# Order of the input projections of a state-space block in a one-core kernel

## The reference, cut to what is computed

```python
zxbcdt = rms_norm(x, ln_g) @ in_w                      # 1024 -> 2048 (z) + 3072 (x, B, C) + 32 (dt)
xbc = silu(causal_dwconv(xbc, conv_w, conv_b))         # 4 taps
y = ssd_chunked(xs * dt, a, bm, cm) + xs * d_skip      # 4 groups of 8 heads, 4 chunks of 128 tokens
y = y * silu(z)                                        # the gate
y = rms_norm(y per group) * norm_g
return y @ out_w
```

## Time and profile before

| | us |
|---|---|
| median of 3 runs (2411.29 to 2411.45) | 2411.38 |
| the profiled execution, device time | 2413.46 |
| its span, from first to last instruction | 2411.7 |
| TensorE busy in the span | 2383.3 |
| VectorE, ScalarE, GpSimd busy | 1404.2, 1054.0, 370.6 |

### The profile page before, as it was taken

The page is one execution under the profiler, slowest core; times in us unless marked ns, Lnnn a source line. Parts: engine busy times, 40 slices in busy tenths (PEclk is TensorE's granted clock), DMA queues, the critical chain, the costliest instruction groups (busy, mean ns, idle before and its releaser), DMA issues.

```text
span 2411.7 us, 29936 instructions
## 1 busy us (share of the span) xinstructions
PE 2383.3 (99%) x11690; PEld 1940.0 (80%) x11690; DVE 1404.2 (58%) x2203; ACT 1054.0 (44%) x1808; POOL 370.6 (15%) x296
## 2 busy tenths in 40 slices
PE   8999999999999999999999999999999999999998
PEld 6677778888888877788888787787788887888887
DVE  6878775763665677766456547535555445443342
ACT  6654564442445677644234334324443333322223
POOL 0352252210111000221011100001211001110001
PEclk9999999999999999999999999999999999999999
DMA  4542223223323221232332332231244322223322
GB/s 163 107 94 79 81 70 101 90 87 110 97 78 128 71 71 54 78 105 90 99 100 83 122 102 74 71 109 58 71 131 127 114 97 88 88 94 100 103 82 85
DMA packets 74270, 226.21 MB, mean 94 GB/s; under 512 B 8081, under 2 KB 12305, under 8 KB 74001
## 3 DMA queue, kind: packets, MB, share of 16 engines
q1 hardware_dynamic: 69696, 215.90, 27.9%
q10 hardware_dynamic: 4432, 8.39, 2.0%
HBM read 215.87 MB, written 8.39 MB: 93 GB/s over the span
## 4 chain that ended last, share of the span: by engine, by line
PE 62%; DVE 1%; issue 0%; ACT 0%; POOL 0%; POOLq 0%; DVEq 0%
PE bank L1161 60%; PE bank L1165 1%; DVE t L2022 0%; DVE t L2019 0%; DVE t L2030 0%; ACT t L1555 0%; DVE t L2026 0%; POOL t L2589 0%; ACT t L1558 0%; POOLq L2808 0%; DVE t L2512 0%; DVEq L2808 0%; DVE t L2358 0%; DVE t L2518 0%; DVEq L770 0%
## 5 line engine op out<-in xcount | busy, mean ns | idle before, releaser
L1161 PE MATMUL bank<-t 128*128 128x512 f32 (+6 forms) x11268 | 2359.4, 375 | 18.7 <-DVE t L2022 7.8
L1161 PEld LDWEIGHTS bank<-t 128*128 128x128 f32 (+2 forms) x11268 | 1897.2, 185 | 450.3 <-issue 80.5
L1555 ACT ACTIVATE t<-t 128x1024 fp32r<-128x1024 f32 (+6 forms) x633 | 539.3, 862 | 676.5 <-PE bank L1161 281.2
L2019 DVE TENSOR_TENSOR t<-t 128x1024 fp32r<-128x1024 f32 (+6 forms) x686 | 623.9, 919 | 251.6 <-ACT t L1555 246.4
L1558 ACT ACTIVATE t<-t 128x512 f32<-128x512 f32 (+6 forms) x609 | 367.2, 617 | 468.2 <-DVE t L2019 312.7
L2589 POOL TENSOR_TENSOR t<-t 128x512 f32<-128x512 f32 (+4 forms) x216 | 329.0, 1530 | 1546.2 <-ACT t L1558 558.4
L2019 DVE TENSOR_TENSOR t<-bank,t 128x512 f32<-128x512 f32 (+4 forms) x410 | 275.1, 675 | 467.5 <-PE bank L1161 457.6
L2022 DVE SCALAR_TENSOR_TENSOR t<-t 128x512 f32<-128x512 f32 (+5 forms) x496 | 368.1, 752 | 101.0 <-ACT t L1558 63.0
L1555 ACT ACTIVATE t<-bank 128x512 f32<-128x512 f32 (+4 forms) x150 | 71.3, 496 | 115.8 <-PE bank L1165 97.7
L2592 POOL TENSOR_SCALAR t<-t 128x128 f32<-128x128 f32 (+3 forms) x64 | 40.9, 645 | 483.1 <-ACT t L1555 252.3
L2022 DVE SCALAR_TENSOR_TENSOR t<-bank,t 128x512 f32<-128x512 f32 x56 | 38.5, 687 | 69.6 <-PE bank L1161 69.6
(11 more groups left out here) (29 smaller groups left out, 42.8 us busy)
## 6 DMA issues: line engine op xcount, KB each, us to landing
t<-in_w SPq DMA_DIRECT2D x304, 512.0 KB, 3.3
t<-in_w SPq DMA_DIRECT2D x48, 384.0 KB, 3.1
t<-in_w SPq DMA_DIRECT2D x56, 320.0 KB, 2.9
t<-in_w SPq DMA_DIRECT2D x28, 256.0 KB, 2.8
tab<-t ACTq DMA_DIRECT2D x1, 2560.0 KB
t<-in_x SPq DMA_DIRECT2D x8, 256.0 KB, 4.8
t<-tab SPq DMA_DIRECT2D x8, 256.0 KB, 3.7
spill<-t ACTq DMA_DIRECT2D x1, 2048.0 KB, 8.5
```

Of the source, the lines that this page charges most:

```text
L1161: return eng.matmul(out, lhs, rhs, start=start, stop=stop, skip_group_check=loose)
L1555: return eng.activation(out, in_, ACT.Copy, scale=scale)
L2019: return eng.tensor_tensor(out, a, b, o)
```

## The change

The bodies of `group_in` and `group_z` become functions for one tile, `conv_in` and `gate_in`, with the same conditions. `both(g, order)` walks a string: an `i` is the next `in` tile of group g, a `z` the next gate of group g-1. The number of tiles and everything behind `gate_in(3, i)` stay.

```diff
         first_two()
-        group_in(0)
+        for i in range(2, 6):
+            conv_in(0, i)
         self.cut_age = 3
-        group_in(1)
-        group_z(0)
-        group_z(1)
-        group_in(2)
+        both(1, "ziziizizii")
+        both(2, "ziziizizii")
         out(0)
-        group_z(2, (0, 1))
-        group_in(3)
-        group_z(2, (2, 3))
-        group_z(3)
+        both(3, "ziiziiziiz")
+        for i in range(4):
+            gate_in(3, i)
         out(1)
         out(2)
```

```diff
+        def both(g, order):
+
+            left = {"i": iter(range(6)), "z": iter(range(4))}
+            for kind in order:
+                if kind == "i":
+                    conv_in(g, next(left["i"]))
+                else:
+                    gate_in(g - 1, next(left["z"]))
```

More of the change, by code:

```diff
@@ L430, in first_two, with conv_in, gate_in @@
                 pass
[L432 to L443, removed]
+        def conv_in(g, i):
+            if g >= 2:
+                before, age = (("pair", (g - 2, 3)), 6) if i < 2 else (("yn", g - 2), 0)
+                self.until(lambda: self.past(*before, age), ("in", g, i))
+            if g == 0 and i == 2:
+                self.start("once", 0)
+                self.feat(("dt",), "ssm_in", 5120, "n1", DC, ncol=32, norm="n1")
+            ft = 16 + 4 * i + g if i < 2 else 4 * g + i - 2
+            self.feat(("in", g, i), "ssm_in", 2048 + ft * P, "n1", DC, norm="n1")
+        def gate_in(g, i):
             if g >= 2:
                 self.until(lambda: self.past("gate", g - 2, 1), ("z", g))
-            for i in which:
-                self.feat(("z", g, i), "ssm_in", (4 * g + i) * P, "n1", DC, norm="n1")
+            self.feat(("z", g, i), "ssm_in", (4 * g + i) * P, "n1", DC, norm="n1")
+        def both(g, order):
[5 more added lines that the diff above has]
+                    gate_in(g - 1, next(left["z"]))
         def out(g):
```

## The result

The new order is slower. Its median is 2418.9 us (2416.43 to 2420.22, 8 runs) against 2411.46 us for the kernel before on the same chip; the ratio on record is 1.0026, with a 95% interval from 1.0018 to 1.0035; it lies nearer to the ratio of the means, 1.0028, than to that of the medians, 1.0031. The executions of the kernel before fall into two groups, near 2411.4 and near 2413.8 us, so its median can move by 2 us with the share of each. The forecast was 2406.6 us, the range ended at 2410.8, and slower had been given 0.05. The profiled execution has a span of 2417.4 us and a device time of 2419.18, against 2411.7 and 2413.46.

What follows compares the result with a forecast made beforehand. TensorE was taken as the bound, busy 2383.3 of 2411.7 us, with 9.61 us of stalls as ceiling. Terms from -4.8, -1.34 and -1.16 to added costs sum to -4.8 us: 2411.38 to 2406.6, range 2403.7 to 2410.8.

Steps and rivals of the forecast that it cites:

- slower: Rival, chance 0.05: a VectorE and GpSimd loop in ticks 65 to 100 slows group 1's four pairs, 3.33 us each; 2417.4 us.
- the last sentence on the ticks: Loads, splits and cuts keep one per 4 ticks; DMA issues on SP keep their order, so no term was given.
- Ticks 49 to 53: Stalls of 5.00 us go as VectorE does 4.4 us less work up to tick 51; 0.2 left, so -4.8 us.
- The 1.21 us at tick 50: Old TensorE stall, ended by ScalarE's copy of the first state, put down to VectorE's late cut, weight load and split.
- Tick 101: The product that group 2's `sta` needs becomes 11 ticks old, so its stall goes: -1.34 us.
- The state copies: Stalls at ticks 76 and 172 go as ScalarE's copies move to 83 and 175: -1.16 us, +0.3 for remaining queues.
- Tick 75: First transposes of group 1's `stb` wait for the product of tick 73, against VectorE's 16.3 us of work: +0.5 us.
- Ticks 86 to 90: Group 1's first pair meets `yn` 0 and two convolved tiles, VectorE needing 22.9 us against TensorE's 21.7: +1.2 us.
- Tick 115: Silu of group 2's last `in` tile has almost no margin, with `gate` 1 now 10 ticks later: +0.1 us.
- Tick 130: The stall of 1.66 us for a bank that VectorE frees late stays, since VectorE's steps there keep their ticks.
- Tick 214: `yn` 3 is 4 ticks later, so its last rest is wanted 2.05 us behind tick 209's shifted work: +0.4 us.
- No table load was added: None was forecast; a rival, chance 0.05, had two more near 58 to 68 us, 2.6 us on ScalarE: 2408.0 us.

Runs made afterwards that it cites:

- e6: Kernel before, with weight unit 15 in its own buffer and loaded ahead of the first bias table's write, units 16 to 18 one place earlier: 2411.58 us, ratio 1.0.
- e11: Kernel before, with the second bias table's source in a free area and each table written in 8 spaced parts: 2413.89 us, ratio 1.0002.
- e10: New order, with the second bias table's source in a free area and each table written in 8 spaced parts: 2410.65 us, ratio 0.9991.
- e9: New order, with only the second bias table's source moved to an area free by then: 2417.7 us, ratio 1.002.
- e3: Kernel before, with only the first call of the new order (group 1's convolved tiles in turn with group 0's gates): 2417.12 us, ratio 1.002.
- e1: New order, with the first bias table's write moved to ticks 93 to 149, in 8 parts of one source row each: 2420.69 us, ratio 1.0035.
- e7: New order, with the first bias table written in 8 parts of 16 rows from all source partitions, ticks 37 to 72: 2418.71 us, ratio 1.0032.
- e5: New order, with weight unit 15 in its own buffer and loaded ahead of the first bias table's write, units 16 to 18 one place earlier: 2416.78 us, ratio 1.0021.
- e12: New order, with weight unit 15 loaded ahead of the table write and the second bias table's source in a free area: 2415.7 us, ratio 1.0013.
- e4: New order with group 1 as before, so only its second and third calls are new; plan two ticks longer: 2421.93 us, ratio 1.004.
- e2: Kernel before, with the first bias table's write moved to ticks 93 to 149, in 8 parts of one source row each: 2421.94 us, ratio 1.0037.
- e8: New order, with 18 matrix multiplies that nobody reads at the start of tick 50, filling TensorE's gap: 2419.05 us, ratio 1.0029.

## Why the prediction was wrong

- **The step that failed** is the last sentence on the ticks: "DMA issues on SP keep their order and are not a term". The order of the issues is kept, but the time of landing is a term of its own, and the trace of before had it, in ScalarE's 1.00 us for unit 15 at 88.37 us. Priced by it, ticks 49 to 53 would have read: however early VectorE is, ScalarE's split starts at 88.37, and with a split of 1.06 and a tap of 0.63 us, less their overlaps, the state's copy can't start before 89.9. It started at 90.30. What is taken from VectorE there wins 0.4 us ahead of tick 50, not the 3.51 of its two stalls. The new order did not even win these 0.4: the issue waits for VectorE's cut of unit 12, which it makes 1.2 us later, and TensorE came to tick 50 0.8 us later than before, and not 3.5 earlier.
- **A wrong reason for a right row.** The 1.21 us at tick 50 were explained with "late because VectorE's cut, hence the next weight load and split, was late". e6 shows taps of VectorE as the cause. And a cut only starts a load; 19.7 us of transfer lay between the two, which no earlier cut shortens.
- **Ticks 49 to 53, -4.8 (bounds -5.0 and -2.5).** VectorE's side was right: at the stall it has been idle for 6.03 us. With the transfers out of the way, e11 has 2.30 + 1.22 + 1.47 = 4.99 us there and e10 0.74, so -4.25. In the change itself it was 4.55 us at tick 50 instead of 5.00 in all, with the lower clock behind it, and 0.48 at tick 55.
- **Tick 101, -1.34:** right; there is no such stall after. **The state copies, -1.16 + 0.3:** both stalls are gone and, in e10, none came at ticks 83 and 175. The 1.15 us at tick 84 of the kernel after is the landing of the tables, a wait that the prediction doesn't name at all: it moved `yn` 0 by 5 ticks and weighed its rounded parts as work on ScalarE, but not what they wait for. ScalarE is ready for them at 155.97 us instead of 169.56, and the writes end at 158 us.
- **Tick 75, +0.5 (0 to 2.3):** 0.82. **Ticks 86 to 90, +1.2 (0 to 3.5):** 0.58 at the first pair; the later pairs of group 1 add 0.70 and 0.64, so 1.92 in all, not over the 3.5 that the prediction named as a limit. **Tick 115, +0.1:** 0.17. **Tick 130** keeps its 1.66. **Tick 214, +0.4:** 0.22, and a stall of 0.36 us at 356 us, ended by VectorE ahead of 64-row products, is one that no term covers.
- **Not on the list:** 0.91 us at tick 64, where the last pair of group 0 now meets convolved tiles and TensorE waits for GpSimd. The prediction looked for such stalls only at group 1's pairs.
- **The sum without transfers.** The prediction's terms give -4.8 us for the whole, and e10 against e11, which differ by the order alone, give 2410.65 - 2413.89 = -3.2, or 188.01 - 190.84 = -2.8 in the stretch. The working was thus right in kind and 1.6 to 2 us too hopeful. The rows of e10 say where: 0.91 us at tick 64, 0.67 more than forecast at the pairs of group 1, 0.54 more at tick 53 and 0.33 more at tick 75, less 0.4 that was set aside at ticks 83 and 115 and did not come. The transfers turned the sign: with them the order costs 5.6 us in the stretch, without them it wins 2.8, so they are worth 8.4.
- **The rivals.** Slower had been tied to a loop between VectorE and GpSimd. The time given for it, 2417.4, is near the result by luck, since its mechanism is not there: the pairs of group 1 cost 1.9 us and not 13.3. No table load was added: both pages count 15.
- Nothing changes clear of the spread behind 410 us: from the row at tick 130 to the end it is 2168.4 us before and 2168.8 after.

## What to carry to other kernels

When an engine's backlog is taken away, list what else the instruction behind it waits for, transfers above all, and when that came in the old trace: a wait of 1.00 us on a load can be the visible end of one that has 7 us behind it. A step moved earlier brings along the waits that guard its destination, here the landing of a write whose source shares the memory. And if a first repair shifts a stall without moving the end, compare the absolute time at which the wait ends in several runs: where it is nearly the same, 157 to 158 us here, it is a floor.

## What the runs showed of the hardware

A stall can cost TensorE its clock, and the length of the stall alone does not tell whether it does. These are mean granted clocks in the 5.5 us behind a stall, 1.00 being full: 0.55, 0.54 and 0.51 behind 4.55, 4.51 and 4.59 us (after, e9, e3), 0.56 and 0.70 behind 7.66 and 7.18 (e1, e7), 0.69 behind 2.36, 2.29 and 2.27 (e5, e12, e4), but full behind 3.34 and 3.49 at 159 us (e5, e12). Behind the same stall of 2.30 or 2.31 us of the old order it was full in the traces of before, e2, e4 and e11, while e6 has 0.69. Keeping the engine busy kept the clock (e8) and won nothing, since ScalarE, held by a transfer, set the pace.

2560 KB written in 8 copies, each from one source row, kept the DMA engines 0.87 to 0.91 busy at 76 to 106 GB/s, loads included, and loads of 512 KB beside them took up to 24.9 us (e1, 190 to 235 us). In e10 the same bytes from 8 source rows in each part, with gaps between the parts, left them at 8.6 or less from 60 to 235 us. The two writes of the tables, 4096 KB, took 86 to 89 us together in every kernel in which the second was written whole behind the first.
